# Memory attention of a streaming encoder layer: keys, values, queries in this order, with the heads' work between the query tiles

## The reference

```python
def memory_kv(mem, g_mkv, w_mk, w_mv):
    m = rmsnorm(mem, g_mkv)
    mk = (m @ w_mk).reshape(B, M, MEM_HEADS, MEM_HEAD_DIM)   # 256 memory tokens, 4 heads x 256
    mv = (m @ w_mv).reshape(B, M, MEM_HEADS, MEM_HEAD_DIM)
...
    mq = (rmsnorm(x, g_xq) @ w_mq).reshape(B, T, MEM_HEADS, MEM_HEAD_DIM)
    s = jnp.einsum('bthd,bmhd->bhtm', mq, mem_k) * (MEM_HEAD_DIM ** -0.5)
    p = jax.nn.softmax(s, axis=-1)
    mo = jnp.einsum('bhtm,bmhd->bthd', p, mem_v).reshape(B, T, D_MODEL)
    x = x + mo @ w_mo
```

## Time and profile before

| | us |
|---|---|
| runs (three) | 954.06, 954.38, 955.01 |
| median | 954.38 |
| span of the profiled execution | 954.0 |
| PE busy | 907.1 |
| DVE busy | 522.8 |
| ACT busy | 358.7 |
| POOL busy | 57.8 |

### The profile page before, as it was taken

How to read it: one execution, slowest core, us unless ns; L and a number is a source line. 1 busy time by engine, 2 the same in 40 slices (tenths; PEclk the granted TensorE clock), 3 DMA queues, 4 the chain that set the end, 5 groups by cost and what they waited for, 6 DMA issues and landing times.

```text
span 954.0 us, 16665 instructions
## 1 busy us (share of the span) xinstructions
PE 907.1 (95%) x6426; PEld 869.8 (91%) x6426; DVE 522.8 (55%) x932; ACT 358.7 (38%) x575; POOL 57.8 (6%) x97
## 2 busy tenths in 40 slices
PE   4999999999899999977999999999999999999996
PEld 3888999989798899866999999999999999999996
DVE  4365666676566343656366756532465643356644
ACT  5254455444634422563234333321233221133323
POOL 4012110041100000012000000000000000000000
PEclk9999999999999999998899999999999999999999
DMA  6236422304332532540032233323223332222222
GB/s 195 58 102 160 112 83 75 90 24 151 123 99 81 168 116 88 188 144 1 22 88 89 67 88 88 88 70 85 77 77 88 88 88 77 78 84 70 71 83 101
DMA packets 116856, 88.83 MB, mean 93 GB/s; under 512 B 3168, under 2 KB 107830, under 8 KB 116819
## 3 DMA queue, kind: packets, MB, share of 16 engines
q1 hardware_dynamic: 111683, 71.15, 25.3%
q0 software_dynamic: 5136, 17.17, 5.9%
HBM read 81.32 MB, written 6.99 MB: 93 GB/s over the span
## 4 chain that ended last, share of the span: by engine, by line
PE 86%; DVE 6%; ACT 5%; issue 2%; DMA 1%; DVEq 0%; ACTq 0%; SPq 0%
PE ps L364 66%; PE ps L1620 3%; PE ps L1729 3%; PE ps L1487 3%; PE ps L1814 2%; PE ps L1548 2%; PE ps L1591 1%; DVE mp L1357 1%; ACT w_hi L375 1%; PE ps L1549 1%; DVE y_tok L1450 1%; PE ps L1554 1%; PE ps L1764 1%; ACT mp L989 1%; PE ps L1473 1%
## 5 line engine op out<-in xcount | busy, mean ns | idle before, releaser
L380 DVE TENSOR_TENSOR w_lo<-w_raw,w_hi 128x1024 fp32r<-128x1024 f32 x124 | 152.5, 1231 | 222.8 <-ACT w_hi L375 220.6
L375 ACT ACTIVATE w_hi<-w_raw 128x1024 fp32r<-128x1024 f32 x124 | 131.0, 1057 | 244.9 <-PE ps L364 206.4
L364 PE MATMUL ps<-b_hi,w_hi 128*128 128x288 f32 x832 | 179.3, 297 | 3.4 <-DVE w_lo L380 1.2
L364 PE MATMUL ps<-b_hi,w_lo 128*128 128x288 f32 x832 | 178.2, 296 | 0.0
L364 PE MATMUL ps<-b_lo,w_hi 128*128 128x288 f32 x832 | 178.1, 296 | 0.0
L364 PE MATMUL ps<-a_hi,w_hi 128*128 128x288 f32 x800 | 173.6, 299 | 0.4 <-DVE w_lo L380 0.4
L364 PE MATMUL ps<-a_lo,w_hi 128*128 128x288 f32 x800 | 171.8, 296 | 0.0
L364 PE MATMUL ps<-a_hi,w_lo 128*128 128x288 f32 x800 | 171.8, 296 | 0.0
L364 PEld LDWEIGHTS ps<-b_hi,w_hi 128*128 128x128 f32 x832 | 134.0, 189 | 4.4 <-issue 1.5
L364 PEld LDWEIGHTS ps<-b_hi,w_lo 128*128 128x128 f32 x832 | 134.1, 189 | 0.0
L364 PEld LDWEIGHTS ps<-b_lo,w_hi 128*128 128x128 f32 x832 | 134.1, 189 | 0.0
(11 more groups left out here) (340 smaller groups left out, 1268.1 us busy)
## 6 DMA issues: line engine op xcount, KB each, us to landing
w_raw<-in_w_up SPq DMA_DIRECT2D x44, 512.0 KB, 3.8
w_raw<-in_w_in SPq DMA_DIRECT2D x16, 512.0 KB, 4.0
w_raw<-in_w_down SPq DMA_DIRECT2D x16, 512.0 KB, 3.8
w_raw<-in_w_o SPq DMA_DIRECT2D x8, 512.0 KB, 3.9
w_raw<-in_w_mk SPq DMA_DIRECT2D x8, 512.0 KB, 3.2
w_raw<-in_w_mq SPq DMA_DIRECT2D x8, 512.0 KB, 3.7
w_raw<-in_w_mv SPq DMA_DIRECT2D x8, 512.0 KB, 3.3
w_raw<-in_w_mo SPq DMA_DIRECT2D x8, 512.0 KB, 3.8
```

The source lines that it names most:

```text
L364: mm = nc.tensor.matmul(acc[:, h, 0:H], w[slot][:, c], x[:, k, h * H:h * H + H], start=(k == first and w is w_hi and x is x_hi), stop=(k = ...
L375: nc.scalar.activation(w_hi[slot][:], w_raw[slot][:], ACT.Copy).then_inc(weight_hi_ready, 1)
L380: nc.vector.tensor_tensor(w_lo[slot][:], w_raw[slot][:], w_hi[slot][:].bitcast(F32), ALU.subtract).then_inc(weight_lo_ready, 1)
```

## The change

The order of the projections becomes keys, values, queries. The value tiles go to ACC[0] and ACC[1], the query tiles to SC and OB. The prompt's keys are turned behind the third value tile. The blocks' scores, turns and values stand in between the query tiles. The low part of the prompt's values is made from the accumulator by DVE, no longer from kv_tok by DVE and POOL, and POOL stores both results before it loads the cached keys. The statistics of the maxima get a tile of their own with two halves (`mem_stat`). The first two output tiles are begun without their last two feature tiles and finished at the end. a_hi, a_lo and b_hi, b_lo swap their parts from the output projection on.

The diff, cut to its core:

```diff
-    W_V, W_QK, W_U, W_O, W_MK, W_MQ, W_MV, W_MO = 0, 4, 12, 16, 24, 32, 40, 48
+    W_V, W_QK, W_U, W_O, W_MK, W_MV, W_MQ, W_MO = 0, 4, 12, 16, 24, 32, 40, 48
...
             by_rows(W_MK, a["w_mk"][0], 0, KT // 2)
+            by_rows(W_MV, a["w_mv"][0], 0, KT // 2)
             by_columns(W_MQ, a["w_mq"][0])
-            by_rows(W_MV, a["w_mv"][0], 0, KT // 2)
...
+            for k in range(KT):
+                round_weights(act, W_MV + 2 + k, k % 2)
+                if k == 2:
+                    memory_keys(0)
...
+            def queries(k):
+                round_weights(act, W_MQ + 2 + k, k % 2)
+                act.wait_ge(acc_free, A_MQ + 1 + k)
+                copy(b_hi[:, k, :], gained[:], MSCALE).then_inc(mq_hi, 1)
...
+            def queries(k):
+                rest_of_weights(dve, W_MQ + 2 + k, k % 2)
+                dve.wait_ge(weight_used, W_MQ + 1 + k)
+                dve.wait_ge(mq_ready, k)
+                nc.vector.tensor_tensor(by_half(gained[:]), halves((SC, OB)[k % 2]), by_half(inv_rms[:]), mult).then_inc(acc_free, 1)
+                dve.wait_ge(mq_hi, k + 1)
+                scaled_minus(b_lo[:, k, :], gained[:], MSCALE, f32(b_hi[:, k, :])).then_inc(mq_ready, 1)
...
+            def queries(k):
+                pe.wait_ge(weight_lo_ready, W_MQ + k + 1)
+                if k < 2:
+                    pe.wait_ge(mk_ready, 2 * k + 2)
+                else:
+                    pe.wait_ge(acc_free, A_MQ + k - 1)
+                project(k % 2, a_hi, a_lo, (SC, OB)[k % 2], range(KT), KT)
+
+            def scores(s):
+                pe.wait_ge(mq_ready, min(2 * s + 2, KT))
...
+            queries(0)
+            queries(1)
+            scores(0)
+            queries(2)
+            pe.wait_ge(ck_landed, 16)
+            pe.wait_ge(ms_exp, 1)
+            memory_keys(1, 0)
+            memory_keys(1, 1)
+            pe.wait_ge(kv_out, 4)
+            pe.wait_ge(kv_lo, MT)
+            memory_keys(1, 2)
+            memory_keys(1, 3)
+            queries(3)
             scores(1)
-
-            pe.wait_ge(kv_out, 4)
             memory_turn(0)
-            for s in range(2, MH + 1):
...
+            queries(4)
+            memory_values(0)
+            queries(5)
+            scores(2)
+            memory_turn(1)
+            queries(6)
+            memory_values(1)
+            queries(7)
+            memory_turn(2)
+            scores(SAMPLE)
+            scores(MH)
+            memory_values(2)
+            memory_turn(SAMPLE)
+            memory_values(SAMPLE)
             memory_turn(MH)
+
+            pe.wait_ge(weight_lo_ready, W_MO + 1)
+            pe.wait_ge(ms_exp, MH + 1)
+            pe.wait_ge(mo_ready, MH)
+            project(0, b_hi, b_lo, ACC[0], range(KT - 2), KT)
             memory_values(MH)
-
-            pe.wait_ge(mo_ready, MH)
-            project_all(W_MO, A_MO, a_hi, a_lo, ready=(mo_ready, MH + 1), late=2)
+            pe.wait_ge(weight_lo_ready, W_MO + 2)
+            pe.wait_ge(mt_ready, MH + 1)
+            project(1, b_hi, b_lo, ACC[1], range(KT - 2), KT)
+            pe.wait_ge(mo_ready, MH + 1)
+            for c in range(2):
+                project(c, b_hi, b_lo, ACC[c], range(KT - 2, KT), KT)
+            project_all(W_MO + 2, A_MO + 2, b_hi, b_lo, rounds=KT // 2 - 1)
```

More of the change, by code:

```diff
@@ L147, in build @@
         stat = place("stat", [P, 64])
+        mem_stat = place("mem_stat", [P, 2, 16])
         phase = here[0]
@@ L945, in residual_steps @@
                         act.wait_ge(gained_ready, k + (first + 1))
-                        copy((a_hi if first == 0 else b_hi)[:, bass.ds(k, 1), :].rearrange("p k t -> p (k t)"),
+                        copy(a_hi[:, bass.ds(k, 1), :].rearrange("p k t -> p (k t)"),
                              gained[:]).then_inc(act_hi_ready, 1)
@@ L964, in _, with kept @@
                                  scale=1.0 / D).then_inc(mem_stat_act, 1)
-            root(1, ACC[1])
             act.wait_ge(mem_stat_dve, 1)
             act.wait_ge(stored, 16 * 8)
+            def kept(t, bank):
+                return copy(kv_tok[:, t, :].rearrange("p (b c) -> p b c", b=2), bank[:], stat[:, 20 + t:21 + t])
+            act.wait_ge(weight_used, W_MK + KT)
             for t in range(MT):
[L970 to L977, removed]
+                kept(t, (SC, OB)[t]).then_inc(kv_out, 1)
             def memory_keys(s):
@@ L1003, in _, with turned_hi @@
[L1003 to L1029, removed]
+            def turned_hi(m):
+                hi, _, w = turned_probs(m)
+                act.wait_ge(mt_done, m + 1)
+                copy(hi[:], ACC[1][:, :, 0:w]).then_inc(mt_hi, 1)
@@ new lines, in _ @@
+            normalise(0)
+            queries(2)
+            memory_keys(1)
+            queries(3)
+            maxima(1)
+            turned_lo(0)
+            normalise(1)
+            queries(4)
+            attended_lo(0)
+            queries(5)
+            maxima(2)
+            turned_lo(1)
+            normalise(2)
+            queries(6)
+            attended_lo(1)
+            queries(7)
+            turned_lo(2)
+            maxima(SAMPLE)
+            maxima(MH)
+            normalise(SAMPLE)
@@ L1392, in _ @@
+            turned_lo(SAMPLE)
+            normalise(MH)
+            attended_lo(2)
+            attended_lo(SAMPLE)
+            turned_lo(MH)
+            attended_lo(MH)
+            residual_steps(W_MO, KT, g_ffn, a_lo, a_hi)
             nc.vector.memset(gate[:, 0:2], 0.0)
@@ L1427, in _ @@
                     dve.wait_ge(hidden_hi, f + 1)
-                    minus(flat(a_lo, i), hidden[:], f32(flat(a_hi, i))).then_inc(hidden_free, 1)
+                    minus(flat(b_lo, i), hidden[:], f32(flat(b_hi, i))).then_inc(hidden_free, 1)
                     rest_of_weights(dve, i * 2 + (W_UP[k] + 3), 1)
@@ L1721, in _, with memory_tile @@
             project_all(W_O + 2, A_O + 2, b_hi, b_lo, rounds=KT // 2 - 1)
-            def memory_tile(n, slot, k, first, last):
+            def memory_tile(n, slot, banks, k):
                 pe.wait_ge(weight_lo_ready, n + 1)
@@ L1728, in memory_tile @@
                         for x, w in ((mem_hi, w_hi), (mem_lo, w_hi), (mem_hi, w_lo)):
-                            ins = mm((SC, OB)[t][:, h], x[:, k, t * P:t * P + P], w[slot][:, h * 512:h * 512 + 512],
-                                     start=(first and x is mem_hi and w is w_hi), stop=(last and w is w_lo))
+                            ins = mm(banks[t][:, h], x[:, k, t * P:t * P + P], w[slot][:, h * 512:h * 512 + 512],
+                                     start=(k == 0 and x is mem_hi and w is w_hi), stop=(k == KT - 1 and w is w_lo))
                 ins.then_inc(weight_used, 1)
@@ L1757, in scores, with memory_keys @@
-            def scores(s):
+                memory_tile(W_MK + k, k % 2, (SC, OB), k)
+            def memory_keys(s, q):
+                for c in range(2):
+                    for t in range(MT):
+                        ins = turn(key_bank(s, q)[:, c * MEM + t * P:c * MEM + t * P + P],
+                                   kv_tok[:, t, (2 * q + c) * P:(2 * q + c) * P + P], ident[:])
+                ins.then_inc(mk_turned, 1)
+            pe.wait_ge(root_done, 1)
+            for k in range(KT):
+                memory_tile(W_MV + k, k % 2, ACC, k)
+                if k == 2:
+                    pe.wait_ge(kv_out, 2)
+                    for q in range(4):
+                        memory_keys(0, q)
@@ L1846, in _ @@
                         pe.wait_ge(sum_ready, KT + 2 + f + 1)
-                    project(c, b_hi, b_lo, ACC[c], [f], KT)
+                    project(c, a_hi, a_lo, ACC[c], [f], KT)
                 if c == 0:
```

222 lines of the change are left out of this document (109 added, 113 removed).

## The result

| | before | after |
|---|---|---|
| median | 954.69 us (4 runs, 954.06 to 956.88) | 971.27 us (4 runs, 969.07 to 972.98) |
| span of the profiled execution | 954.0 | 968.5 |

The change is slower: ratio 1.016, 95% interval 1.013 to 1.019, +16.6 us between the medians. The forecast was +13.6, 968.0.

What follows compares the result with a forecast made beforehand. TensorE, busy 907 of 954.0 us, was taken as the bound. Costs 19.2 + 3.3 + 2.8 + 1.7 + 6.4 + 4.0 = 37.4, less 23.8 got back, gave +13.6, 968.0 us; range 960 to 975.

Steps and rivals of the forecast that it cites:

- Query waits: PE stops ahead of the scores for the query tile's low part: three times 5.0 us, once 4.2, together 19.2.
- g: Length of one PE stop between a query tile's last matmul and its usable low part: 5.0 us.
- Clock behind them: Half clock in the scores and query tile after each of four query waits: 1.6 us each, 6.4 in all.
- c: Time lost to half clock after one query wait: 1.6 us, bounds 0 and 1.6.
- Projections: Key and value tiles back to back wait on weight buffers, key copies and the store: 3.3 us, bounds 0.4 and 7.
- The starving rival: Value stage: store and two loads collide, waits above 2 us bring half clock; 7 us, total 973, chance 0.10.
- The sample's values: The sample's light 64-column matmuls in the tail still lose clock: 4.0 us, bounds 0 and 8.
- The rival with s = 0: Clock holds through the sample's values, no loss there; total 964.0, chance 0.20.
- Tail: Waits ahead of the sample's turn, its values and the output projection: 2.8 us, between 0 and 5.2.
- the output projection's wait on x_t: Output tile 2 waits for rounding, split and addition of tile 0: 1.7 us.
- the 23.8: Idle PE time and half clock of before, mostly in memory attention, that could be got back: 23.8 us, leaving 930.6.
- Faster: Rival: query tile usable in 2.5 us without the weight ahead, no clock lost; total 947.6, chance 0.04.

Runs made afterwards that it cites:

- e1_split_last: Changed kernel with the weight's rounding and split put behind the tile's own gain, copy and low part in odd query tiles; 957.2 us, ratio 1.0025.
- e2_one_moved: Changed kernel with only the third head's scores one query tile later, between query tiles 6 and 7; 963.3 us.
- e3_filled: Changed kernel with 36 overwritten 128 x 256 matmuls in each wait before the scores of heads 0, 1 and 2; 965.2 us.
- e5_kept_late: Changed kernel with ScalarE's two key copies to kv_tok behind the rounding of the third value weight; 967.4 and 973.1 us.
- e11_key_early: e8_best with the third key weight's rounding and split ahead of the last residual tile's copy and low part; 937.4 us.
- e10_mixed: e6_sample_filled with one overwritten 128 x 256 matmul behind each of 16 groups of three narrow ones in the sample's values; 946.8 us.
- e9_gathered: Changed kernel with attention gathered behind the eight query tiles, scores alternating between two banks and narrow scores of the sample; 949.1 us, ratio 0.992.
- e6_sample_filled: e4_moved with 12 overwritten 128 x 256 matmuls in the wait before the sample's values; 943.6 us.
- e4_moved: Changed kernel with the scores of heads 0, 1 and 2 each one query tile later; 948.6 us, ratio 0.992.
- e7_moved_narrow: e4_moved with e1_split_last's edit, the sample's scores reading 64 query columns and standing ahead of the third head's turn; 946.0 us, ratio 0.989.
- e8_best: e7_moved_narrow plus the edits of e5_kept_late and e6_sample_filled, third head's probabilities rounded earlier, residual addition before the weight's split; 937.3 us, ratio 0.981.

## Why the prediction was right

The sign and the mechanism held, and the size nearly: there are four query waits with half clock behind them, and the median is 3.3 us above the forecast. Part of that is luck, since terms that were too low and too high cancel. The total is taken from start to start, since a matmul's record outlasts the start of the next. From the first key tile (300.35) to the third output tile (489.97) after takes 189.6 us, and before 174.7 (300.72 to 475.4): 15.0 more.

- **Query waits: 18.4, said 19.2.** From 353.80 to the scores at 371.48 are 17.68 us, less two tiles of 6.41 this is g = 4.86; the other three are 4.85, 4.78 and 3.92. e1_split_last shows the first two links of the chain as the forecast had them, e2_one_moved the price of one wait.
- **Clock behind them: 9.2, said 6.4.** This term was mis-sized. I took c = 1.6 from the 3.3 us at half clock of the earlier trace rows and made it the upper bound. The scores exceed 2.83 us by 2.07, 1.92 and 2.46, and the last pair exceeds 5.66 by 2.78. e3_filled gave back 6.2 of the first three's 6.45 (6.1 by the medians). In the earlier trace rows half clock lasted 3.3 us; here, by the matmuls' starts, it lasted 4.2, 4.0, 5.3 and 6.1 us from each wait's end.
- **Projections: 3.1, said 3.3.** After's stage takes 53.45 us (300.35 to 353.80). The like pieces of before are 27.63 (to 328.35) and 24.1 of value tiles and key turns between 379.63 and 408.66, 51.7 in all, and 1.4 of that was half clock which this execution of after didn't have behind its 2.0 us wait. The wait before the third value tile was said to be 1.7 and was 1.36, and e5_kept_late removes it. The 1.6 that I took for the store meeting the next loads was not seen: the only wait there is 0.29 us, at 344.39. The rest is the 0.42 us wait ahead of the first query tile and short steps, so that the term came near by luck. The starving rival's waits of over 5 us did not come.
- **The sample's values: 4.9, said 4.0.** The values took 7.62 us against 5.34 at full clock (e11_key_early; 0.111 us a matmul, where the forecast's sign had half of 0.21, 0.107), the turn 1.69 against about 0.8 as behind scores 1 and the output part 6.60 against 4.85 in e10_mixed. Bounds 0 and 8 hold it, and the runs span much of them: 5.34 us for the values in e11_key_early and 9.84 in e9_gathered; 4.0 was the middle of a wide range, and that it came near is luck. That the clock can fall behind this work without a long wait, e6_sample_filled, e10_mixed and the trace of after show. The rival with s = 0 does not fit: the wait before the values was 1.41 us in after and none in e6_sample_filled, and the clock fell in both. The rule of the Trainium skill, "TensorE: Matmul & The Clock Gate", section "Why this matters for your kernels", is that the clock drops if PE pauses for more than about 3 us between bursts. These executions don't fit it, and neither does e1_split_last, where 2.36 us cost the clock twice.
- **Tail 1.6, said 2.8**, with the output projection's wait on x_t 1.7, said 1.7. The waits of 0.5 ahead of the sample's turn and 0.7 ahead of the output projection, both estimates, did not come.

I had booked the 0.4 us wait ahead of the first query tile as got back, and it is there again at 353.80. These make 3.1 - 1.4 + 0.4 + 18.4 + 9.2 + 4.9 + 1.6 + 1.7 = 37.9, less the 23.8: 14.1. The remaining 0.9 us I can't place. Then there is the step from the span to the time. I set what lies around the span to 0.4, from a span and a median of different executions; in the profiled executions of the runs here it was 1.7 to 1.8 (970.3 for a span of 968.5), and 1.7 to 2.2 over all runs of the kernel before beside them. The forecast span, 967.6, was 0.9 short of 968.5; this step makes 1.4 more, and the median lies another 1.0 above the profiled execution: 3.3 in all.

What the forecast missed is not a term but the two halves of the change. I priced the order of the projections only as a cost (+3.3) and booked what it brings under the whole. e9_gathered shows the changed kernel without the interleaving (with two banks for the scores and narrow scores of the sample) at 949.1, faster than before, and e4_moved shows that the interleaving is free if each head's scores stand one tile later. The rival *Faster* named the right thing: in e1_split_last the weight stands behind the tile and g falls to 2.5 us, but behind two of the three longest waits the clock still fell, and the kernel took 957.2, not 947.6.

## What to carry to other kernels

On an in-order engine, put the consumer of a tile at least one full tile behind it, and on the engines that drain it serve the tile before the weight that is needed later: the first edit took 22.6 us from this kernel, the second, made alone, 14.1. Price a wait on TensorE with the clock behind it: here 4.65 us of waiting cost 7 to 8. When a change has two halves, build each alone before judging it.

## What was not expected of the hardware

- A wait of the same length is answered differently. Within one execution, 2.36 us was followed by a granted clock of 0.64, 1.00 and 0.62 in the scores of e1_split_last. Between executions, the wait before the third key tile was followed by half clock in before (2.12 us, then 7.13 for two tiles) and by full clock in after (2.02, then 5.70). What decides it stays open; no run here varied only that.
- Code before 300 us, which neither of two runs changes, varies between executions by the clock alone. Two stretches of it, columns as above, in e6_sample_filled and then in e7_moved_narrow:
```profile
60.00:80.00 20.00, 17.88 (x124) 16.25 (x123) 12.51 (x23) 8.70 (x18) 6.20 (x10) 1.00 0.53 135
80.00:95.00 15.00, 15.00 (x108) 13.60 (x107) 10.23 (x33) 8.37 (x22) 1.71 (x2) 1.00 0.44 110
```
```profile
60.00:80.00 20.00, 17.88 (x107) 17.06 (x107) 10.88 (x18) 8.20 (x15) 6.20 (x10) 0.81 0.51 133
80.00:95.00 15.00, 15.00 (x82) 12.56 (x82) 6.87 (x25) 5.86 (x18) 0.91 (x1) 0.80 0.41 101
```
The mean clock of these 35 us is 1.00 in one and 0.81 in the other, by an estimate from the matmuls done (189 against 232) some 6 to 7 us. It is most of why the profiled run of e7_moved_narrow took 954.0 us while its other four took 944.4 to 947.1, and why differences under 2 us were read from the traces here, not from medians.
- Behind short matmuls the granted clock fell even where PE never stopped: 48 of 64 columns, back to back, ran at 0.53 in e9_gathered, 0.72 in e8_best and, in the same order, at 1.00 in e11_key_early (5.34 us, with 0.77 in the stretch behind). They and that stretch ran at 1.00 in the profiles of both runs with a 256-column one behind every three. Each number is from one execution.
